# Modulation vectors of a two-layer encoder step: shift and scale of layer 0 made ahead of it, all others made in the projection tiles' spare PSUM columns

## What is computed

```
def modulate(x, c, g, w_ada, b_ada):
    mod = jnp.dot(jax.nn.silu(c), w_ada) + b_ada         # w_ada: 2048 x 6144
    shift, scale, gate = jnp.split(mod, 3, axis=-1)
    h = rmsnorm(x, g) * (1 + scale[:, None]) + shift[:, None]
    return h, gate[:, None]
...
    h, gate = modulate(x, c, g_n, w_a, b_a)
    xa, za, qb, kb, vb, zb, qc, kc, vc, zc, qi, ki, wi = project(h, w_i)
    ...   # RG-LRU over 8 blocks, band attention and sparse attention of 4 heads each
    out = merge(hs, ob, oc, za, zb, zc, gbr, w_o)
    return x + gate * out, new
```

## Time and profile before

| | us |
|---|---|
| median of 3 runs | 2644.24 (2638.18 to 2647.77) |
| the profiled execution | 2642.81 |
| its span | 2641.0 |
| PE busy | 2413.8 (91%) |
| PE weight loads | 2148.1 (81%) |
| DVE, ACT, POOL busy | 997.4, 818.5, 870.1 |
| bytes read from HBM | 280.81 MB |

### The profile page before, as it was taken

How to read it: one execution, slowest core, us unless ns; L and a number is a source line. 1 busy time by engine, 2 the same in 40 slices (tenths; PEclk the granted TensorE clock), 3 DMA queues, 4 the chain that set the end, 5 groups by cost and what they waited for, 6 DMA issues and landing times.

```text
span 2641.0 us, 52419 instructions
## 1 busy us (share of the span) xinstructions
PE 2413.8 (91%) x16711; PEld 2148.1 (81%) x16711; DVE 997.4 (38%) x1784; ACT 818.5 (31%) x1546; POOL 870.1 (33%) x651
## 2 busy tenths in 40 slices
PE   5669999999999999879977899999999999996998
PEld 2128889989999989779922688999999999886997
DVE  2342347775112233431115333677621122354113
ACT  0023334443333324322201233444433333333221
POOL 5023224334333323334401322333333333342441
PEclk6559999999999999989965899999999999997999
DMA  8982222223333322234499422222233323222443
GB/s 311 371 300 67 60 64 71 76 72 91 95 92 86 82 78 78 59 106 128 123 331 382 129 56 63 68 78 72 75 100 92 90 79 84 74 77 72 129 128 134
DMA packets 410102, 311.75 MB, mean 118 GB/s; under 512 B 21304, under 2 KB 347840, under 8 KB 408712
## 3 DMA queue, kind: packets, MB, share of 16 engines
q1 hardware_dynamic: 382296, 283.35, 35.6%
q10 hardware_dynamic: 27632, 26.21, 3.2%
HBM read 280.81 MB, written 30.92 MB: 118 GB/s over the span
## 4 chain that ended last, share of the span: by engine, by line
issue 62%; POOL 22%; PE 8%; DMA 5%; POOLq 1%; DVE 0%; SPq 0%; DVEq 0%; ACT 0%; ACTq 0%
POOL w_lo L460 21%; DMA work<-in_w_ada 5%; PE proj L575 2%; PE proj L571 2%; PE proj L569 2%; POOL act_lo L453 1%; PE misc L515 1%; POOLq L467 1%; POOLq L459 0%; DMA raw<-in_w_in 0%; DMA out_y_prompt<-work 0%; DVE work L1162 0%; DMA raw<-in_x_prompt 0%; DVE xy L1182 0%; PE misc L491 0%
## 5 line engine op out<-in xcount | busy, mean ns | idle before, releaser
L569 PE MATMUL proj<-act_hi,w_hi 128*128 128x288 f32 (+1 forms) x4672 | 1336.1, 301 | 29.4 <-DVE act_lo L1159 20.2
L571 PE MATMUL proj<-act_lo,w_hi 128*128 128x288 f32 (+1 forms) x4672 | 1313.6, 297 | 0.0
L460 POOL TENSOR_TENSOR w_lo<-raw,w_hi 128x512 fp32r<-128x512 f32 (+1 forms) x584 | 780.4, 1340 | 1414.0 <-ACT w_hi L869 1413.7
L575 PE MATMUL proj<-act_hi,w_lo 128*128 128x288 f32 (+1 forms) x4672 | 1003.7, 296 | 0.0
L569 PEld LDWEIGHTS proj<-act_hi,w_hi 128*128 128x128 f32 (+1 forms) x4672 | 886.0, 190 | 58.3 <-issue 47.3
L571 PEld LDWEIGHTS proj<-act_lo,w_hi 128*128 128x128 f32 (+1 forms) x4672 | 885.6, 190 | 3.6
L575 PEld LDWEIGHTS proj<-act_hi,w_lo 128*128 128x128 f32 (+1 forms) x4672 | 754.0, 189 | 0.0
L869 ACT ACTIVATE w_hi<-raw 128x512 fp32r<-128x512 f32 (+1 forms) x584 | 365.5, 629 | 1166.6 <-PE proj L575 1133.9
L515 PE MATMUL misc<-work,sc 128*2 128x512 f32 x768 | 166.9, 969 | 80.0 <-DMA work<-in_w_ada 73.9
L515 PEld LDWEIGHTS misc<-work,sc 128*2 128x2 f32 x768 | 14.9, 87 | 195.9 <-issue 195.6
L453 POOL TENSOR_TENSOR act_lo<-xy,act_hi 128x576 fp32r<-128x576 f32 x32 | 50.2, 1582 | 289.5 <-ACT act_hi L876 232.3
(11 more groups left out here) (172 smaller groups left out, 1716.1 us busy)
## 6 DMA issues: line engine op xcount, KB each, us to landing
raw<-in_w_in SPq DMA_DIRECT2D x448, 256.0 KB, 2.8
work<-in_w_ada SPq DMA_DIRECT2D x96, 1024.0 KB, 8.6
raw<-in_w_out SPq DMA_DIRECT2D x128, 256.0 KB, 2.7
x_keep<-xy ACTq DMA_DIRECT2D x32, 288.0 KB, 2.5
lb<-x_keep SPq DMA_DIRECT2D x24, 288.0 KB, 3.2
x_keep<-xy ACTq DMA_DIRECT2D x4, 1152.0 KB, 10.9
out_y_prompt<-work SPq DMA_DIRECT2D x4, 1024.0 KB, 3.9
qi_raw<-x_keep SPq DMA_DIRECT2D x8, 288.0 KB, 3.8
```

Of the source, the lines that this page charges most:

```text
L460: pool.tensor_tensor(w_lo[:, c, :, 0:width], raw[:, c, :, 0:width], w_hi[:, c, :, 0:width].bitcast(F32), ALU.subtract)\
L569: pe.matmul(dst, w_hi[:, c, kk, 0:width], act_hi[:, k, cols], start=(k == 0), stop=False)
L571: pe.matmul(dst, w_hi[:, c, kk, 0:width], act_lo[:, k, cols], start=False, stop=False)
L575: m = pe.matmul(proj[b][0:width, half, 0:HALF], w_lo[:, c, kk, 0:width], act_hi[:, k, cols], start=False, stop=(k == KT - 1))
```

## The change

Nothing that is computed changes; where and when the modulation is made does.

- The small vectors of both layers are loaded, turned and kept at the start (`vec1_of`, `vec2_of`, `sp_of` and so on, one for each layer).
- Ahead of layer 0 only 8 blocks of `w_ada` are loaded, in another order: a quarter of the shift, the same quarter of the scale, and so on. After each pair DVE adds the bias and scales four k-tiles; the chunks of KI, whose weights come earlier, stand between the blocks on PE.
- The rest (layer 0's gate, layer 1's shift, scale and gate) is made in pieces of 256 columns: 24 pieces in the QI and LRU tiles of layer 0, 8 in the QI tiles of layer 1. For a piece SP loads 2 MB in two transfers to the upper half of `xy` (`late_w`); PE does it in two halves (`late_unit`), one ahead of chunk 2, one ahead of chunk 3, into columns 288 to 415 of the tile's banks; DVE copies the rows out with the tile (`late_take`); PE turns them in the next tile (`late_turn`, into columns 420 to 423), and DVE adds the bias one tile later.
- Ahead of layer 1 there is no modulation left. DVE multiplies with scale and `r_x` in one instruction and adds the shift in a second.
- In the recurrent blocks DVE's order is `best` twice, `late_take`, `convolve(g)`, `recur(g - 1)`, `gate_path`, `late_take`; `convolve` writes one of two buffers, `lb[1]` or `ki_t`.
- ACT copies layer 1's KI weights ahead of the 16 copies to `act_hi`, and layer 0's behind the first four; POOL splits them at the same places.
- The loops over tiles are written out, and `hold` no longer counts `ticks` where its value is a constant. ACT no longer waits for the blocks (`ada_used`) before it stores x to HBM.

```diff
+AW = 256
+AT = D_MODEL // AW
+LATE = (3 * AT, AT)
+LATE_AT = (0, 3 * AT)
+A_ROW, A_MOD = HALF, HALF + 132
...
+            def load_late(l, i):
+
+                layer, col = (l, 2 * D_MODEL + AW * i) if i < AT else (l + 1, AW * (i - AT))
...
+                for u in range(2):
+                    if n > 0:
+                        hold(sp, late_used, 2 * n + u - 1)
+                    sp.dma_start(late_w[:, u], w[:, u * 8:u * 8 + 8, col:col + AW]).then_inc(late_in[u], 16)
...
+            hold(pe, x_whole, 1)
+            sum_squares(proj[0], sqx)
...
+                def late_unit(i, u, b):
+
+                    n = LATE_AT[l] + i
+                    hold(pe, late_in[u], 16 * (n + 1))
+                    for r in range(2):
+                        for half in range(2):
+                            for kk in range(KC):
+                                k = r * KC + kk
+                                m = pe.matmul(proj[b][32 * kk:32 * kk + 2, half, A_ROW:A_ROW + P],
+                                              sc[:, u * 8 + k, :], late_w[:, u, k, half * P:(half + 1) * P],
+                                              start=False, stop=(u == 1 and r == 1),
+                                              tile_position=(0, 32 * kk), skip_group_check=True)
+                    m.then_inc(late_used, 1)
...
+                def late_turn(i, b):
+
+                    n = LATE_AT[l] + i
+                    hold(pe, late_read, n + l + 1)
+                    for d in range(2):
+                        m = pe.matmul(proj[b][:, 0, A_MOD + 2 * d:A_MOD + 2 * d + 2],
+                                      late_row[n % 2][:, d * P:(d + 1) * P], sel[:, :],
+                                      start=False, stop=True, skip_group_check=True)
+                    m.then_inc(late_turned, 1)
...
+                if l == 0:
+                    modulate(4)
+                    modulate(5)
+                    turn_modulation(4)
+                    turn_modulation(5)
+                    chunks(KI, 0, 0, (0,), 80, acts=0)
+                    modulate(6)
+                    chunks(KI, 0, 0, (1,), 80, acts=0)
+                    modulate(7)
+                    turn_modulation(6)
+                    turn_modulation(7)
+                    chunks(KI, 0, 0, (2, 3), 80, acts=0)
+                else:
+                    hold(pe, x_whole, 2)
+                    hold(pe, bank_free[0], l * USES[0])
+                    sum_squares(proj[0], sqx)
+                    chunks(KI, 0, 0, range(4), 80, acts=0)
...
+                else:
+                    for k in range(KT):
+                        for a, z, w in PARTS:
+                            stt(xy[:, k, a:z], xy[:, k, a:z], mod[:, KT + k, w:w + 1], r_x[:, a:z],
+                                ALU.mult, ALU.mult)
+                        dve.drain()
+                        for a, z, w in PARTS:
+                            dve.tensor_scalar(xy[:, k, a:z], xy[:, k, a:z], mod[:, k, w:w + 1], None, ALU.add)
+                        dve.drain().then_inc(norm_x, 1)
+                        if k % 2 and k > 1:
+                            lower(k - 2, 0)
...
                 def recurrent_block(g, first=False):
+                    for _ in range(2):
+                        best((1, 2, 3), P)
...
+                        late_take(AT + 2 * g, 1)
+                    convolve(g)
                     if not first:
                         recur(g - 1)
-                    convolve(g)
-                    for _ in range(2):
-                        best((1, 2, 3), P)
                     gate_path(LRU + 1 + 2 * g, 0, tile(xy, g))
```

More of the change, by code:

```diff
@@ L343, in _ @@
[L343 to L351 removed]
+                    sp.dma_start(vrow_of[l][row:row + rows, int(n > 6), :], src).then_inc(vec_in, 16)
@@ L353, in _ @@
+            for l in range(DEPTH):
                 w_in = inp["w_in"][l].rearrange("(k p) n -> p k n", p=P)
@@ L462, in split @@
                         .then_inc(lo_ready, 1)
-            with pool.Fori(0, DEPTH) as l:
-                lower(l, 0)
-                split(l, KI, 80)
+            for l in range(DEPTH):
+                if l == 0:
+                    lower(l, 0, 0, KC)
+                    split(l, KI, 80)
+                    lower(l, 0, KC, KT)
+                else:
+                    split(l, KI, 80)
+                    lower(l, 0)
                 with pool.Fori(1, OUT + 1) as t:
@@ L632, in _ @@
                 query_tile(1, 0, 1, True)
-                with pe.Fori(0, 3) as it:
+                for it in range(3):
                     query_tile(2 * it + 2, 1, it + 1)
@@ L661, in recurrent_block @@
                         t_event(2)
-                    chunks(LRU + 1 + 2 * g, 0, g + 5, range(4))
+                    chunks(LRU + 1 + 2 * g, 0, g + 5, (0, 1))
+                    late(AT + 1 + 2 * g, 0, 0)
+                    chunks(LRU + 1 + 2 * g, 0, g + 5, (2,))
+                    late(AT + 1 + 2 * g, 1, 0)
+                    chunks(LRU + 1 + 2 * g, 0, g + 5, (3,))
                 recurrent_block(0, True)
-                with pe.Fori(1, G) as g:
+                for g in range(1, G):
                     recurrent_block(g)
@@ L848, in _ @@
             act.wait_ge(rel_out, 48)
-            with act.Fori(0, DEPTH) as l:
-                hold(act, vec_ready, l + 1)
-                act.activation(sp_[:, 0, :], vec1[:, V1["lam"]:], ACT.Abs)
-                act.drain()
-                act.activation(sp_[:, 0, :], sp_[:, 0, :], ACT.Exp, scale=-1.0)
-                act.drain().then_inc(lam_exp, 1)
+            decay(1)
+            for l in range(DEPTH):
+                sp_, hb = sp_of[l], hb_of[l]
                 def root(r, n):
@@ L934, in _ @@
                 query_tile(1, 0, True)
-                with act.Fori(0, 3) as it:
+                for it in range(3):
                     query_tile(2 * it + 2, 1)
@@ L994, in _ @@
                 recurrent_block(0, True)
-                with act.Fori(1, G) as g:
+                for g in range(1, G):
                     recurrent_block(g)
@@ L1168, in _ @@
             dve.memset(selm[0:CHUNK, CHUNK:P], NEG)
+            for n in range(2):
+                for half in range(2):
+                    dve.memset(proj[n][:, half, A_ROW:A_MOD + 4], 0.0)
+            dve.drain().then_inc(psum_clear, 1)
             dve.wait_ge(vec_made, 1)
@@ L1349, in _ @@
                 add_scores(0)
-                with dve.Fori(0, 3) as it:
+                for it in range(3):
                     query(2 * it + 1, 0)
```

372 lines of the change are left out of this document (236 added, 136 removed).

## The result

| | before | after |
|---|---|---|
| median, us (4 runs each, one chip) | 2642.26 (2638.18 to 2647.77) | 2561.61 (2559.48 to 2563.81) |
| ratio, with its 95% interval | | 0.9694 (0.9673 to 0.9714) |
| span of the profiled execution | 2641.0 | 2559.7 |
| instructions in the trace | 52419 | 46975 |

The change makes the kernel 81 us faster.

The account below looks back on a forecast made before the run. PE was taken as the bound, except in the two modulation stretches, where DMA was. Terms -40 - 97 - 24 - 8 + 86 + 36 + 8 = -39 took 2642.8 to 2604 us, range 2562 to 2668.

Parts of the forecast that it names:

- rival 3: Pieces' transfers: no late loads at all, since SP is ahead; the 36 and the 8 go, 2560 us; chance 0.08.
- the two signs: The prediction fails if a half of a piece takes over 1.55 us, or layer 1's start over 80 us.
- The order, 24 and 8: Recurrent blocks: convolution starts earlier, so the gates' wait goes, -24 us; clock comes back in layer 1, -8 (0 to 12).
- Layer 0's start, 40: Start up to QI of layer 0: fewer blocks loaded ahead, QI begins at 166 instead of 206.6; 40 us less (30 to 48).
- I take 3: Layer 0's start: 3 us (0 to 8) for DVE taking first blocks behind decay vectors, which wait for ACT and bias windows.
- Layer 1's start, 97: From x whole to QI of layer 1: a chain without modulation remains, 59 us instead of 156; 97 less (90 to 104).
- The pieces, 2.7 each: 32 modulation pieces on PE: two halves 1.9 us, turn 0.53, switches 0.25; 86 us added in all.
- lower bound of 74: Pieces on PE: total cost of all 32 if the halves run at the streaming bound, 74 us.
- Rival 1: Pieces on PE: records start no faster than 0.06 us apart, a half takes 1.95, +64: 2668 us; chance 0.16.
- Late loads, 36 and 8: Layer 0's LRU tiles: loads land 3.2 us late in xa, 2.0 in za; 36 us (10 to 60), plus 8 clock.
- the za tile lasts 12.6 without additions: Recurrent blocks: with za tiles of 12.6 us, ACT comes free 5 us into the next tile.
- The terms of the move: Modulation's move: layer 0's start -40, layer 1's start -97, pieces 86, late loads 36, their clock 8 us.

Follow-up runs that it names:

- b_order: Kernel before with its tile loops written out, waits for constants not counted, and DVE's new order in the recurrent blocks: 2559.83 us, ratio 0.9709.
- b_nocount: Kernel before with its loops over layers, query tiles and recurrent blocks written out and waits for constants not counted: 2566.19 us, ratio 0.9733.
- a_front: Changed kernel with layer 1's exponential made right behind layer 0's, and rows of blocks 4 to 7 copied out when there: 2541.85 us, ratio 0.9642.
- a_late3: Changed kernel with the pieces' loads issued one chunk earlier in SP's order in the recurrent tiles: 2548.04 us, ratio 0.9661.
- a_twice: Changed kernel with the 32 records of each half of a piece done twice: 2619.28 us, ratio 0.9929.
- a_narrow: Changed kernel with 32 moving columns instead of 128 in the pieces' matmuls: 2525.03 us, ratio 0.9582.
- b_loops: Kernel before with only its loops over layers, query tiles and recurrent blocks written out, every wait still counted: 2594.89 us, ratio 0.9836.

## Why the prediction was half right

By spans the change won 81.3 us: 41.3 by written-out loops, 35.3 by waits not counted, 8.4 by the order on DVE, and the move of the modulation lost 3.8. By the ratios, where the medians of several runs stand, it is 43, 27 and 6 us, and the move won 4; the intervals of b_order and of the changed kernel lie over each other. So **the move by itself, as it was made, is not told from nothing**, and nearly all of the gain is in a line of the change that the prediction listed nowhere.

- **The step that failed is a missing term.** The part of the prediction that goes through the change edit by edit names the modulation, the order, the pieces and their transfers, and leaves out the loops and `ticks`. They were worth 70 us, 77 by spans. With the 39 of the sum that makes 116, and not 81: the order and layer 0's start won 24 and 23 us less than they were priced at, and the other terms some 12 more. So it is luck that the time is only 0.4 us below the range, and also that it lies 2 us from rival 3's 2560: that rival has no late loads, and the trace has 19.3 us of them. Neither of the two signs that the prediction named for its failure came up (a half takes 0.87 us and not over 1.55, layer 1's start 55 and not over 80). The rows were there: `<-issue` behind a wait on DVE, and a wait of 16.9 us for the copies of the scores. An edit that touches every wait of every engine needs a price even when it computes nothing.
- **The order, 24 and 8.** That the wait goes was right, but the loops and the counting took 19.5 of its 23.7 us (4.2 stay in b_nocount), and the order added 6 to 8. And the size was too small in another way: the prediction gave the clock back in layer 1 only and counted 32, where the LRU tiles of both layers lose 44.4 from before to b_order. Twelve waits of 2.0 us stood for up to 3.7 us each, if all that these tiles lost is put down to them.
- **Layer 0's start, 40.** Measured 24.8, and 17.3 against b_order, which already has the shorter chains. The step was "I take 3" for DVE's order. It has two places, 26.0 us of DVE's waiting for an exponential and 13.0 us of PE's waiting for rows; without them QI begins 7.9 and 15.1 us earlier. a_front shows that the rest of the working was sound: 158.9 where 166 was worked out, and the 7.5 us that loops, counting and order give this stretch (206.6 to 199.1) were not in it.
- **Layer 1's start, 97.** Measured 102.1 from before, and 90.9 from b_order. QI begins 55 us behind the end of the layer instead of 59. About 11 us of the 102 are loops and counting.
- **The pieces, 2.7 each.** Against b_order: 24.5 / 8 and 23.9 / 8 in query tiles, 47.3 / 16 in the LRU tiles of a_late3, so 3.0 each and 96 in all, where the sum had 86. But 7.1 us of the 96 are waits for the pieces' loads. A tile without such a wait shows the piece alone: in a_late3 an xa tile takes 17.4 us and a za tile 15.4, in b_order 14.6 and 12.6. That is 2.8 a piece, and the price was right. The half at the streaming bound was right too (0.82 in a_twice, 0.95 forecast). What is left of 2.8 for the switches is 2.8 less 2 x 0.86 less 0.53, 0.55, where 0.25 stood; that is an estimate from these rows and was not measured alone. The prediction's lower bound of 74 doesn't follow from its own terms: 2 x 0.86, 0.53 and 0.25 are 2.5 a piece, 80.
- **Rival 1, records started no faster than 0.06 apart, is out.** 32 records of 32 columns start within 0.22 us in a_narrow, 0.007 apart. The Trainium skill, "TensorE: Matmul & The Clock Gate", section "Wait — 56ns, not 53.3ns?", has about 62 ns for each MATMUL with hardware decode off; by that these 32 would take 2.0 us. The trace shows that this rate does not hold here; whether hardware decode was on, no run shows. The 0.16 that hung on it is settled.
- **Late loads, 36 and 8.** Measured 19.3 us of waits in all, and 17.3 us for the LRU tiles with their clock. The za tiles are as forecast (1.9 for 2.0). The xa tiles have one wait of 0.7, where 3.2 each were forecast, and the first two query tiles of each layer have 4.4 in all, where none was forecast. The step was "the za tile lasts 12.6 without additions": in layer 0 it has additions and lasts 17.4, so `recur` is done inside it; and `hs_ready` comes 13.0 us behind the end of the xa tile, where 16.8 were worked out. ACT squares its states at 483.53, 4.3 us ahead of the next xa tile, and not 5 us into it:

```profile
483.53 0.63 ACT L1089 ACTIVATE sq<-lb 128x512 f32<-128x512 f32 x1 [5.84 <-DVEq L1583]
```

- **The terms of the move add up to -7 in the prediction** (-40, -97, 86, 36 and 8), and by the spans to +3.8. Its parts were off by up to 27 us and made up for each other.

What stays open: what part of a loop's cost is its register work and what part is its branch and what comes with it, which were not taken apart; what the order on DVE, or the move, would give on the kernel before with its loops and counts, since each was run only behind them; and whether the changed kernel without its flaws would win more by putting fewer pieces into LRU tiles, which was not tried.

## What to carry to other kernels

A rewrite that turns loops into written-out code, or takes an instruction out of every wait, is an edit with a price of its own: count the steps of the chain that the bound engine waits for, and take the idle `<-issue` ahead of each. Price what is moved against the kernel with everything else of the change already in it, since a shorter chain may leave a new order nothing to win. And when bytes are the bound, look for the engine whose small copy frees the buffer: 0.7 us of work stood behind 13 us here and stopped the transfers for 15.

## What was not expected of the hardware

- A counted wait isn't free. Behind two of them a DVE step starts 0.41 us late, 0.34 with the loop written out, and 0.19 without the counts; the trace has 2770 instructions fewer in b_nocount than in b_loops, and the kernel is 29 us faster. The Trainium skill, "VectorE: DVE Perf Modes", section "Rules for kernel authors", says to "Minimize op *count*, not sems". That is told of an increment which rides on an operation; here the increment is an instruction by itself between a wait and the operation behind it, and 29 us hang on it.
- Four column groups of the array start a pass of 32 columns each 0.03 us (8 passes within 0.22), so that pieces this narrow still stream.
- A window with waits of 2.0 us on PE shows a granted clock of 0.95, the same one with waits of 0.31 shows 1.00, and the LRU tiles of layer 0 with waits of 0.9 show 1.00 where they had 0.97. The tiles win almost twice what the waits lasted (44.4 for 23.7 us, the shorter chains at other places included).
